# Adding up the conditioning sections: transposed 32x32 blocks on VectorE and one product on TensorE

## The reference, cut to what matters

```python
c_act = jax.nn.silu(c)
for l in range(DEPTH):
    mod = (c_act @ ada_w[l] + ada_b[l])[:, None, :]
    sh1, sc1, g1, sh2, sc2, g2 = jnp.split(mod, 6, axis=-1)
    h = rmsnorm(x, norm_mix_w[l]) * (1.0 + sc1) + sh1
    x = x + g1 * hybrid_mixer(h, ...)
    h = rmsnorm(x, norm_ffn_w[l]) * (1.0 + sc2) + sh2
    x = x + g2 * (swiglu(h, ...) if l == 0 else moe_swiglu(h, ...))
return rmsnorm(x, final_norm_w)
```

## Time and profile before

| | us |
|---|---|
| runs, median (lowest, highest) | 1497.26 (1496.41, 1498.6) |
| profiled execution, its own time | 1496.42 |
| its span, first to last instruction | 1494.9 |
| PE busy | 1482.9 (99%) |
| DVE busy | 1278.4 (86%) |
| ACT busy | 955.0 (64%) |
| share of the chain that ended last: PE, DVE | 48%, 1% |

### The profile page before, as it was taken

One profiled execution on the slowest core, in us unless ns is written; L12 is line 12 of the kernel. 1 busy time (PEld: TensorE's weight loads), 2 busy tenths in 40 slices (PEclk: granted clock), 3 DMA queues, 4 the chain that ended last, 5 costly groups with the idle time before them and its releaser, 6 DMA issues. The chain is left out here.

```text
span 1494.9 us, 24158 instructions
## 1 busy us (share of the span) xinstructions
PE 1482.9 (99%) x8409; PEld 1301.9 (87%) x8409; DVE 1278.4 (86%) x1504; ACT 955.0 (64%) x1135; POOL 42.7 (3%) x73
## 2 busy tenths in 40 slices
PE   9999999999999999999999999999999999999997
PEld 8999889999999999889988888888888888888886
DVE  5999688777766799587799999999999999999998
ACT  3635345444535535345688787888878888788885
POOL 5000000000000000000010000000000000000100
PEclk9999999999999999999999999999999999999999
DMA  9956599388994756498399999999999999999993
GB/s 349 314 167 232 199 324 302 127 299 297 382 409 161 230 164 231 143 326 305 117 400 401 410 393 405 365 385 401 362 397 369 382 403 362 397 366 383 411 393 137
DMA packets 208410, 470.88 MB, mean 315 GB/s; under 512 B 16156, under 2 KB 89044, under 8 KB 208340
## 3 DMA queue, kind: packets, MB, share of 16 engines
q1 hardware_dynamic: 204576, 457.27, 83.5%
q0 software_dynamic: 3488, 12.59, 2.1%
q10 hardware_dynamic: 276, 0.09, 0.0%
HBM read 454.69 MB, written 15.21 MB: 314 GB/s over the span
## 5 line engine op out<-in xcount | busy, mean ns | idle before, releaser
L1282 ACT ACTIVATE split<-raw 128x1024 fp32r<-128x1024 f32 x748 | 778.9, 1061 | 293.7 <-PE psU L691 137.6
L2089 DVE TENSOR_TENSOR split<-raw,split 128x1024 fp32r<-128x1024 f32 x528 | 616.9, 1219 | 22.8 <-ACT split L1282 10.5
L691 PE MATMUL psU<-split,yS 128*128 128x512 f32 x2448 | 564.6, 390 | 0.1
L691 PEld LDWEIGHTS psU<-split,yS 128*128 128x128 f32 x2448 | 457.9, 188 | 94.9 <-DVE split L2089 0.7
L1549 DVE TENSOR_TENSOR split<-raw,split 128x1024 fp32r<-128x1024 f32 x220 | 262.2, 1220 | 81.7 <-ACT split L1282 81.0
L691 PE MATMUL psU<-hS,split 128*128 128x256 f32 x2400 | 293.4, 284 | 0.5 <-DVE hS L1747 0.5
L691 PEld LDWEIGHTS psU<-hS,split 128*128 128x128 f32 x2400 | 289.8, 192 | 1.2 <-issue 0.6
L691 PE MATMUL psA<-split,hidE 128*128 128x512 f32 x1056 | 246.0, 392 | 0.0
L691 PEld LDWEIGHTS psA<-split,hidE 128*128 128x128 f32 x1056 | 196.4, 188 | 40.2
L691 PE MATMUL psU<-split,hS 128*128 128x512 f32 x816 | 190.1, 390 | 0.0
L691 PEld LDWEIGHTS psU<-split,hS 128*128 128x128 f32 x816 | 152.2, 188 | 31.3
(11 more groups left out here) (275 smaller groups left out, 837.7 us busy)
## 6 DMA issues: line engine op xcount, KB each, us to landing
raw<-in_moe_w_dram SPq DMA_DIRECT2D x496, 512.0 KB, 5.9
raw<-in_w_in_dram SPq DMA_DIRECT2D x114, 512.0 KB, 5.8
raw<-in_ada_w_dram SPq DMA_DIRECT2D x96, 512.0 KB, 7.2
raw<-in_ffn_w_dram SPq DMA_DIRECT2D x66, 512.0 KB, 8.1
raw<-in_moe_w_dram SPq DMA_DIRECT2D x64, 256.0 KB, 6.3
raw<-in_w_o_dram SPq DMA_DIRECT2D x16, 512.0 KB, 5.5
token_rows<-sc SPq DMA_DIRECT2D x11, 512.0 KB, 12.8
raw<-in_w_br_a_dram SPq DMA_DIRECT2D x8, 512.0 KB, 5.8
```

The costliest lines, as they stand in the source:

```text
L691: return pe.matmul(o, a, b, start=start, stop=stop, skip_group_check=True)
L1282: return act.activation(o, i, ACT.Copy)
L2089: TTN(split[:, slot, 1, :], raw[:, (RAW0 + n) % RAW, :], split[:, slot, 0, :].bitcast(F32), ALU.subtract).then_inc(s_lo, 1)
```

## The change: what it does

DVE transposes a finished accumulator in place, in 32x32 blocks, and then sums each block's 32 columns (`fold`). Of 128 x 1024 numbers 128 x 32 are left (`red`, two of them in turn): partition 32i+r holds in column j the sum over the 32 partitions of group i, for the section's number 32j+r. One product on PE with a fixed 128 x 128 matrix `comb` (identity blocks of 32, built at the start on DVE) adds the four groups, and leaves the sum in all four groups of partitions. `modulate` then takes its numbers with four small additions, one for each group, where it took one. The product waits for a new semaphore, `section_blocks_folded`.

The places move too. Section 6l+2 stays. Sections 6l+4 and 6l+3 are summed ahead of the last quarter of `wo` and used before the norm. Section 5 stays, and 7 and 6 are summed together behind the tenth pair of the dense channel mixer. Only section 11 stays at layer 1's first norm. `stream` products take some of the places left in the norms.

```diff
-            def ada_sum(s, bank=None, ks=range(KD)):
-                pe.wait_ge(s_afree, ADA_DONE[s])
+            def ada_sum(s, bank=None):
+                pe.wait_ge(s_fold, FOLD_AT[s] + 1)
                 ...
-                acc = accumulator(s)
-                for k in ks:
-                    last = mm(bank[:, k * WIDE:(k + 1) * WIDE], acc[:, k * P:(k + 1) * P], ones[:, 0:WIDE], True, True)
+                col = WIDE if s in FOLLOWS else 0
+                last = mm(bank[:, col:col + 32], comb[:, :], red[FOLD_AT[s] % 2], True, True)
 ...
+            def fold(s):
+                acc = accumulator(s)
+                dve.wait_ge(s_afree, ADA_DONE[s])
+                link(dve.transpose(acc, acc))
+                settle()
+                dve.tensor_reduce(red[FOLD_AT[s] % 2], acc.rearrange("p (j q) -> p j q", q=32), axis=AX_X,
+                                  op=ALU.add).then_inc(s_fold, 1)
 ...
+                        if (n, j) == (0, 3):
+                            fold(6 * l + 2)
+                        if (n, j) == (1, 3):
+                            fold(6 * l + 3)
 ...
                 for j in range(4):
+                    if j == 1:
+                        fold(6 * l + 4)
+                    if j == 3:
+                        modulate(6 * l + 4)
+                        modulate(6 * l + 3)
                     bank = unit((l, "wo", j))
 ...
                         done += 1
+                        if done % KD == 0:
+                            fold(FFN_ADA[done // KD - 1])
 ...
             def norm(l, second):
                 if second:
                     low_parts(SIGNAL[l, "wo", 3][2] + AHEAD)
-                    modulate(6 * l + 4)
-                else:
-                    modulate(NORM_SUMS[0])
                 dve.wait_ge(s_eA, ...)
                 link(dve.reciprocal(rstd[:, :], rstd[:, :]))
-                modulate(6 * l + 3 if second else NORM_SUMS[1])
 ...
+                        if j == 3:
+                            ada_sum(6 * l + 4, scale)
+                            ada_sum(6 * l + 3, scale)
                         wo[j] = open_unit((l, "wo", j))
 ...
                     if pair == FFN_SUM_AT:
                         ada_sum(FFN_ADA[0])
+                    if pair == PAIR_AT:
+                        ada_sum(FFN_ADA[1], ada_sum(FFN_ADA[2]))
```

More of the change, by code:

```diff
@@ L82 @@
 DOWN_ADA = [11]
-NORM_SUMS = [7, 6, 11]
+LATE_SUM = 11
+PAIR_SUMS = [(4, 3), (10, 9), (7, 6)]
+LEADS = [lead for lead, _ in PAIR_SUMS]
+FOLLOWS = {follow: lead for lead, follow in PAIR_SUMS}
 LAST_ROWS = 3
@@ L89 @@
 assert sum(FFN_TAKE) == KD * len(FFN_ADA)
+FOLD_AT = {s: n for n, s in enumerate(ADA_ORDER[2:])}
+PAIR_AT = NF // 2 - 2
 FFN_SUM_AT = next(p for p in range(NF // 2) if sum(FFN_TAKE[:p + 1]) >= KD) + 1
@@ L119, in unit_plan @@
         if l == 0:
-            plan += [(("ffn", j), "D") for j in range(NF)] + [(("mod", s), "D") for s in NORM_SUMS]
+            plan += [(("ffn", j), "D") for j in range(NF)] + [(("mod", LATE_SUM), "D")]
     plan += [(("xtok", j), "A") for j in range(3)] + [("logits", "D")]
@@ L332, in program @@
         ix8 = sb("ix8", [P, 2, 8], U32)
+        comb = sb("comb", [P, P])
+        red0 = sb("red0", [P, 32])
         ov = sb("ov", [P, 8, NE * JEX])
@@ L361, in program @@
         scale_acc = work[:, 3, :]
-        norm_acc = {s: merged[:, 4 * n:4 * n + 4, :].rearrange("p a b -> p (a b)") for n, s in enumerate(NORM_SUMS[:2])}
+        red = [red0[:, :], total[:, :, :].rearrange("p a b -> p (a b)")[:, 0:32]]
         factor = work[:, 7, 0:T].rearrange("p (t m) -> p t m", t=TT)
@@ L992, in mixer, with dense_ffn @@
                 stat_sum(stat, 2 * l)
-                ada_sum(6 * l + 4, scale)
+                first = open_unit(("ffn", 0)) if l == 0 else None
+                if l == 0:
+                    stream(first, FILL_SQUARES)
                 stat_pair(stat, 2 * l + 2, 3)
-                ada_sum(6 * l + 3)
-            def dense_ffn():
+                return first
+            def dense_ffn(first):
                 for pair in range(NF // 2):
-                    banks = [open_unit(("ffn", 2 * pair + m)) for m in range(2)]
+                    banks = [open_unit(("ffn", 2 * pair + m)) if pair + m else first for m in range(2)]
                     for which in range(2):
@@ L1086, in _ @@
                          ident[0:NB_ROWS, 0:NB_ROWS]).then_inc(s_unit, 1)
-            mixer(0)
-            dense_ffn()
+            dense_ffn(mixer(0))
             mixer(1)
@@ L1605, in product @@
                 if k == 0:
[L1606 to L1610, removed]
+                    if s == 2:
+                        dve.wait_ge(s_ev, EVENT_AT[("half", 1)] + 1)
+                    elif s % 6 != 4:
+                        dve.wait_ge(s_fold, FOLD_AT[s])
                     TS(acc, raw[:, pos % RAW, :], cact[:, 0:1], None, ALU.mult).then_inc(s_afree, 1)
@@ L1618, in modulate @@
                 l, part = s // 6, s % 6
-                unit_sum = s in NORM_SUMS
-                if unit_sum:
+                late = s == LATE_SUM
+                col = WIDE if s in FOLLOWS else 0
+                if late:
                     dve.wait_ge(s_unit, SIGNAL["mod", s][1])
-                bank = psU[UNIT_AT["mod", s] % 4] if unit_sum else event(("ada", s))[0]
-                dst = mod[:, l, 8 * part:8 * part + 8]
-                sums = bank[:, :].rearrange("p (k r) -> p k r", r=WIDE)[:, :, 0]
@@ L1625, in modulate @@
-                TTN(dst, sums, vecs[:, ADA_B + 8 * s:ADA_B + 8 * s + 8],
-                    ALU.add).then_inc(s_uD if unit_sum else s_eD, 1)
+                bank = psU[UNIT_AT["mod", s] % 4] if late else event(("ada", FOLLOWS.get(s, s)))[0]
+                for c in range(4):
+                    own = slice(32 * c, 32 * c + 32)
+                    sums = bank[own, col:col + 32].rearrange("p (m c) -> p c m", c=4)[:, c, :]
+                    ins = TTN(mod[own, l, 8 * part:8 * part + 8], sums, vecs[own, ADA_B + 8 * s:ADA_B + 8 * s + 8], ALU.add)
+                    if c < 3 or s in LEADS:
+                        link(ins)
+                    else:
+                        ins.then_inc(s_uD if late else s_eD, 1)
@@ L2058, in _ @@
                     done += 1
+                    if done == KD:
+                        fold(DOWN_ADA[0])
             dve.wait_ge(s_eD, emptied(EVENTS, EVENT_AT[("ada", 5)], "D"))
```

47 lines of the change are left out of this document (28 added, 19 removed).

## The result

The changed kernel takes 1512.22 us (median of 5 runs, 1511.35 to 1515.03) against 1496.88 us before: ratio 1.0107, 95% interval 1.0096 to 1.0119. That is slower by 15.3 us, above the range of the prediction (to 1508.0). The profiled execution took 1511.35 us, 14.9 us more than that of before.

A forecast was written before the change was run, and what follows sets the result against it. PE was taken to set the time, every new wait of it paid in full. 3.7 + 1.1 + 2.1 - 0.5 = +6.4 us on 1497.26 us gave 1503.7 us; range 1502 to 1505.6, 8 in 10 from 1499.6 to 1508 us.

The forecast's parts named there:

- The fold's price: Transpose and reduction on DVE at 1.22 us each, 2.44 us for a fold; ends kept: 1.5 and 4.9 us.
- Branch "a": Both layers: PE's sum waits for the fold between DVE's two blocks; next branch 1.85 us later each, +3.7 us together.
- the rival of a dear fold: A fold of 4.9 us: +16.3 us, 1513.6 us; a lower clock behind PE's wait named but not priced; chance 0.10.
- Layer 0's second norm: Fold and small additions during `wo` bring the last block of `xT` 1.5 us later; 0.4 us come back: +1.1 us.
- the 1.9 us of idle time that I counted as free: DVE's idle times of 1.4 and 0.5 us during layer 0's `wo`, set against the added fold and small instructions.
- The dense mixer: Section 5's sum saves PE 1.5 us, which vanish in a wait at pair 10 behind section 7's fold: +2.1 us.
- The wait at pair 10: Section 7's fold ahead of four low parts: the first ready 2.1 us after PE came to it before.
- The folds behind pairs 2 and 5 fall into gaps of that kind: Dense mixer: these folds fall into DVE's waits for transfers, like the 2.12 us one for ACT's copy of a piece.
- Layer 1's norms: First norm: the reciprocal no longer waits behind section 7's bias, -0.5 us; second norm: 0.
- PE's busy time: Over the whole kernel, lower by some 10 us and the span still longer.
- the prediction's own formula: With f for a fold, four terms: twice (f - 0.6), (f - 1.35) while positive, (f - 0.35) and -0.5.
- the ends of its ranges: Own range, f from 2.0 to 2.9 us: 4.8 to 8.3 us more; 8 in 10: 1499.6 us (cheap fold) to 1508 us.

The follow-up runs named there:

- e1_fill: The changed kernel with six `stream` products in PE's wait for the fold behind both branches "a", the wait itself staying; 1507.19 us.
- e5_ffn2: e3_ffn with the small additions of sections 7 and 6 one low part earlier in DVE's list; 1508.69 us.
- e4_wo: The changed kernel with the fold of section 6l+4 ahead of the last two `merged_low` instead of in `wo`; 1508.56 us.
- e3_ffn: The changed kernel with the dense mixer's folds (sections 5, 6, 7) and PE's product for sections 7 and 6 moved later; 1516.34 us.
- e2_early: The changed kernel with the fold of section 6l+2 two places earlier in DVE's list, in DVE's idle time; 1499.35 us.
- e6_all: e2_early, e4_wo and e5_ffn2 together, with layer 0's section 3 `modulate` ahead of the reciprocal and its additions behind `xT`'s last block; 1496.99 us.
- e8_pad: The changed kernel with three `stream` products (1.4 us) behind PE's product for section 5; 1511.93 us.
- e11_late: e6_all with the experts' clearing transfers 14 pieces later and the last section's eight conditioning pieces two behind each of pairs 6 to 9; 1492.76 us.

## Why the prediction was wrong

**The fold's price was right.** 1.24 us for the transpose and 1.22 us for the reduction make 2.46 us, forecast 2.44. The Trainium skill's "VectorE: DVE Perf Modes", section "The perf-mode tier table", gives a reduction the single rate; the trace agrees, with 1.22 us as for the subtraction of two tensors.

**Branch "a": the wait was right, its price was not.** PE waited 3.24 us, forecast some 3.2, and the next branch started 1.9 and 2.1 us later, forecast 1.85. The step that failed is the one that priced this wait by its length alone: the lower clock was left to the rival of a dear fold and named as unpriced. It came at this wait already. The products behind cost 1.6 and 2.6 us more, and 1.5 us more behind pair 10: 5.7 of the 8.5 us that were missing. e1_fill shows this for both branches; for pair 10 it is read from the granted clock of 0.53 alone. It does not come each time: e5_ffn2 has the same wait in layer 1 with the clock at 1.00. The Trainium skill's "TensorE: Matmul & The Clock Gate", Part 1, has the throttled state as the default, released by activity. The traces here agree in that the clock fell where PE idled and rose again with PE at work; the rule bore on this wait too, and not only on the dear fold's.

**Layer 0's second norm: mechanism right, size off.** +2.4 us, forecast +1.1. DVE's last block of `xT` starts at 275.85 us for 269.36, some 2.7 us later beyond the 3.7 us carried in, forecast 1.5. The nine small instructions take 1.74 us (271.72 to 273.46 us), where I had put 1.0. And of the 1.9 us of idle time that I counted as free, 0.52 us is still there (267.94 us): it ends on a copy of ACT's that stands behind the square of a block which DVE, with the fold ahead, brings late (its square, at 266.32 us, waits 2.75 us for it).

**The dense mixer.** The wait at pair 10 came, 1.40 us for section 7's fold itself and 0.59 us for the low part behind it. Section 5 and pairs 9 and 10 together cost 2.65 us without the lower clock, forecast 2.1. "The folds behind pairs 2 and 5 fall into gaps of that kind" was wrong: those gaps are the landing time of pieces that DVE itself has released. What SP waited for at a slot's release, in the changed kernel and in the same stretch of the kernel before:

```profile
SPq L523 <- DVE adacc L1630: 8.5, 1, 8.5
```

```profile
SPq L514 <- DVE merged L1611: 6.8, 1, 6.8
```

Both are the first product of section 7, which stands behind section 6's fold now, and behind four small additions for section 5 (0.73 us) where there was one: SP waits 1.7 us longer, the pieces that it fetches then land later, and so come the low parts made from them. In the kernel before, the first low part of pair 9 was ready at 381.28 us:

```profile
380.06 1.22 DVE L1549 TENSOR_TENSOR split<-raw,split 128x1024 fp32r<-128x1024 f32 x1
```

PE began the pair at 382.45: 1.2 us to spare, less than the 1.55 us that PE saved at section 5. So pair 9 was late by 1.35 us, and the saving was mostly gone. This is read from the two traces. No run moved section 6's fold alone, and pair 9's wait differs widely between the profiles: none in e4_wo, 0.80 us in e3_ffn, 3.36 in e5_ffn2.

**Layer 1's norms.** -0.4 us forecast -0.5 in the first; +0.3 us forecast 0 in the second.

Taken without the clock, the places add up to 9.0 us: on 1497.26 us some 1506.3 us, inside the range. Of the rivals, the dear fold came near in its time (1513.6 us) and for its second reason, not its first. PE's busy time, forecast some 10 us lower, rose by 1.3: the `stream` products and the slower products, 15.7 us together, outweigh the 14.8 us that the sums save. By the prediction's own formula the ends of its ranges are 4.6 and 8.2 us for its 4.8 and 8.3, and 1499.9 us for its 1499.6; nothing hangs on that.

## What to carry to other kernels

Price a wait of the matrix engine twice: by its length, and by the products behind it at the lower clock. Give the second as a range: behind one and the same wait of 3.24 us it was nothing in one profile and 2.6 us in another. An engine's idle time is only free if what ends it does not hang on that engine's own earlier work: follow who released the thing waited for. Moving one fold two places up in a fixed list was worth nearly as much as the whole loss.

## What the runs showed of the hardware that was not expected

The granted clock fell to the 1.2 GHz level behind PE's idle times of 3.24 us, behind two of 1.40 and 0.59 us close together in the dense mixer, and behind 2.06 us at e2_early's pair 9. The length alone does not decide it. Layer 1's 3.24 us left it at 1.00 in e5_ffn2, and 2.36 us at pair 9 did in e6_all. The 2.59 us of layer 0's second norm left it at 1.00 in the changed kernel's profile, but not in e8_pad's (PE, then the stretch behind):

```profile
278.56 1.73 PE L700 MATMUL psA<-sig,ones 128*128 128x256 f32 x4 [2.59 <-ACT sig L1360]
```

```profile
279.00:282.30 3.30, 3.30 (x10) 2.59 (x9) 1.63 (x2) 1.42 (x2) 0.00 (x0) 0.50 0.43 143
```

What decides is not shown. In e4_wo's profile it was still 1.00 from 181 to 182 us, with PE at work again behind layer 0's wait, and 0.50 from 183 us on. So runs of one kernel can scatter with it, as e6_all's do; e11_late, which has none of these waits, has all nine runs within 0.9 us at 0.998 to 0.999.

The dense mixer's pace hung on single pieces: 18 us between two ways of spreading the same 24, folds and clock included.
